# Expert layer of a two-block transformer kernel: upper 256 tokens computed densely, lower 256 by gathered rows

## The reference, cut to what matters

```
s = einsum('thpd,hpnd->thpn', q, sub_keys)          # 128 keys on each of two sides
sc, idx = top_k(s, 16)                              # best 16 of each side
cand = sc[..., 0, :, None] + sc[..., 1, None, :]    # 256 pair sums of a head
top_sc, pos = top_k(cand, 16)                       # best 16 pairs = experts
gate = softmax(top_sc)
act = gelu(einsum('thkd,td->thk', u_tab[eb], hb))   # 128 experts of each token
y = einsum('thk,thkd->td', gb * act, v_tab[eb])
```

## Time and profile before

| what | value |
|---|---|
| median of 3 runs | 3458.14 us (3454.32 to 3459.94) |
| span of the profiled execution, first to last instruction | 3452.1 us |
| busy: PE, DVE, POOL, ACT | 3142.6, 2087.5, 1917.9, 1062.6 us |
| DMA, moved in all | 741.7 MB, of it 536.9 MB by the gathers |
| DMA in the last third of the span | 421 GB/s, all 16 engines busy |

### The profile page before, as it was taken

The page is one execution under the profiler, slowest core; times in us unless marked ns, Lnnn a source line. Parts: engine busy times, 40 slices in busy tenths (PEclk is TensorE's granted clock), DMA queues, the critical chain, the costliest instruction groups (busy, mean ns, idle before and its releaser), DMA issues.

```text
span 3452.1 us, 34902 instructions
## 1 busy us (share of the span) xinstructions
PE 3142.6 (91%) x12254; PEld 2099.6 (61%) x12254; DVE 2087.5 (60%) x3701; ACT 1062.6 (31%) x2577; POOL 1917.9 (56%) x1198
## 2 busy tenths in 40 slices
PE   7999999999999999999999999999978787777776
PEld 5778778887766888868777677544433333333332
DVE  5764453336764433479556776777667676666654
ACT  4564441112165211120132432333333332333222
POOL 4545259997403899968767565444444444434432
PEclk9999999999999999999999999999999999999999
DMA  4430022232311222323413124999999999999997
GB/s 164 171 134 1 13 86 98 97 120 74 134 62 49 90 95 96 115 71 124 140 62 115 50 80 172 421 421 419 422 415 412 421 421 421 421 421 420 421 421 299
DMA packets 108994, 741.68 MB, mean 215 GB/s; under 512 B 11816, under 2 KB 12968, under 8 KB 20776
## 3 DMA queue, kind: packets, MB, share of 16 engines
q0 software_dynamic: 73728, 536.90, 37.5%
q1 hardware_dynamic: 31488, 196.25, 16.2%
q10 hardware_dynamic: 3624, 6.56, 0.5%
HBM read 731.28 MB, written 8.39 MB: 214 GB/s over the span
## 4 chain that ended last, share of the span: by engine, by line
PE 63%; DMA 21%; DVE 8%; ACT 4%; issue 2%; POOL 2%; DVEq 0%; POOLq 0%; ACTq 0%
DMA arena<-in_peer_uv,rstd 15%; PE bank L1298 13%; PE bank L1299 13%; PE bank L1300 13%; PE bank L1814 8%; DMA weight_ring<-in_peer_uv,rstd 3%; DMA normed<-in_peer_uv,rstd 2%; DVE arena L3295 2%; PE bank L1829 1%; PE bank L1744 1%; PE bank L1726 1%; PE bank L1612 1%; PE bank L1490 1%; PE bank L1245 1%; PE bank L1500 1%
## 5 line engine op out<-in xcount | busy, mean ns | idle before, releaser
L1155 POOL DMA_INDIRECT arena<-in_peer_uv,rstd x419 | 456.4, 1089 | 622.0 <-PE bank L1814 570.3
L3295 DVE CUSTOM_DVE_ANT_0 arena<-arena,branch 128x1024 f32<-128x1024 f32 x419 | 510.5, 1225 | 333.5 <-DMA arena<-in_peer_uv,rstd 327.5
L1300 PE MATMUL bank<-split_arena 128*128 128x512 f32 x1776 | 695.1, 391 | 0.0
L1066 POOL TENSOR_TENSOR split_arena<-weight_ring,ones 128x1024 fp32r<-128x1024 f32 x204 | 506.6, 2483 | 151.0 <-PE bank L1300 99.3
L1298 PE MATMUL bank<-split_arena 128*128 128x512 f32 x1392 | 546.6, 393 | 5.6 <-DVE split_normed L2697 2.5
L1299 PE MATMUL bank<-split_arena 128*128 128x512 f32 x1392 | 542.3, 390 | 0.0
L1068 POOL TENSOR_TENSOR split_arena<-weight_ring,split_arena 128x1024 fp32r<-128x1024 f32 x204 | 519.3, 2545 | 16.0
L1814 PE MATMUL bank<-arena,row_diagonals 128*128 128x512 f32 x836 | 397.8, 618 | 92.0 <-ACT row_diagonals L2425 91.7
L1814 PE MATMUL bank<-arena,level_mask 128*128 128x512 f32 x840 | 392.0, 608 | 75.0 <-ACT level_mask L2425 74.7
L1300 PEld LDWEIGHTS bank<-split_arena 128*128 128x128 f32 x1776 | 334.0, 188 | 73.6
L1035 POOL TENSOR_TENSOR split_arena<-weight_ring,split_arena 128x1024 fp32r<-128x1024 f32 x54 | 129.5, 2406 | 401.2 <-ACT split_arena L1980 349.3
(11 more groups left out here) (490 smaller groups left out, 4921.4 us busy)
## 6 DMA issues: line engine op xcount, KB each, us to landing
weight_ring<-in_w_up SPq DMA_DIRECT2D x32, 1024.0 KB, 4.9
weight_ring<-in_w_down SPq DMA_DIRECT2D x32, 1024.0 KB, 4.9
weight_ring<-in_w_in SPq DMA_DIRECT2D x32, 1024.0 KB, 5.0
weight_ring<-in_ada_w SPq DMA_DIRECT2D x24, 1024.0 KB, 4.9
weight_ring<-in_w_in_a SPq DMA_DIRECT2D x12, 1024.0 KB, 6.4
weight_ring<-in_w_out SPq DMA_DIRECT2D x12, 1024.0 KB, 6.9
weight_ring<-in_w_in_b SPq DMA_DIRECT2D x10, 1024.0 KB, 5.9
arena<-in_peer_uv,rstd POOLq DMA_INDIRECT x419
```

Of the source, the lines that this page charges most:

```text
L1066: pool.tensor_tensor(hi, part, bc_mid(ones[:], DT), ALU.mult).then_inc(split_hi, 1)
L1155: pool.indirect_dma_start(row_slots[slot_of[r]], None, a["peer_uv"], bass.IndirectOffsetOnAxis(ap=experts[n % 2][:, c:c + 1], axis=0)).the ...
L1300: return pe.matmul(psum[t.bank][:], hi, a_lo[k], start=False, stop=last)
L3295: dve.tensor_tensor_reduce(row, row, h_tok[:, r // NE, :], 1.0, 0.0, ALU.mult, ALU.add, dots[:, i % 4, j:j + 1]).then_inc(dot_ready, 1)
```

## The change

Blocks 0 and 1 (the lower 256 tokens) still gather rows, 256 in all. Blocks 2 and 3 (the upper 256) are computed against the whole table, which is streamed in 256 *items* of 0.5 MB: 128 items of `u_tab`, transposed (an *up* item: 128 experts by 1024), and 128 of `v_tab` (a *down* item). An up item gives the gelu inputs of 128 experts for 256 tokens (24 fp32r products of 256 columns), a down item adds 128 experts' outputs (12 fp32r products of 512 columns). Most gates are zero; the gate matrix is made from one-hot vectors by small products (64 *gate steps*).

For every item ACT copies the raw data to the high half, and the low half is made by POOL (two items of three) or DVE (every third). Three pairs of halves and four raw buffers rotate.

The order is written out as 320 steps: 64 up items (stage A), 32 gate steps (G0), 128 items in turn down and up (stage B), 32 gate steps (G1), 64 down items (stage C). The first 64 gathered rows are still summed on PE in 32 groups ahead of that (stage S), with all of the queries and 61 pieces of search among them. The other 192 rows are spread over the 320 steps (24 in A, 12 in G0, 96 in B, 12 in G1, 48 in C), and their second half is now added by DVE (`late_add`) in place of PE. Eight searches are left for stage A, one piece a step.

The residual is stored to DRAM and fetched back at the end, since its space holds the split items.

```diff
+        for s, (kind, v) in enumerate(STEPS):        # TensorE
+            if kind == "gate":
+                gate_products(v)
+            elif ITEMS[v][0]:
+                down_unit(v, ITEMS[v][1])
+            else:
+                up_unit(v, ITEMS[v][1])
...
+            def up_unit(n, j):
+                t = u_tiles[j]
+                hi, lo = [x.rearrange("p (k i) -> p k i", i=NKEY) for x in pairs_of[n % PAIRS]]
+                low_wait(pe, n)
+                free(pe, t)
+                for k in range(DT):
+                    pe.matmul(psum[t.bank][:, 0:DENSE], hi[:, k, :], dense_hi[:, k, :], start=k == 0, stop=False)
+                    pe.matmul(psum[t.bank][:, 0:DENSE], hi[:, k, :], dense_lo[:, k, :], start=False, stop=False)
+                    m = pe.matmul(psum[t.bank][:, 0:DENSE], lo[:, k, :], dense_hi[:, k, :], start=False, stop=k == DT - 1)
...
+            def raw_top(n):                          # ScalarE
+                act.wait_ge(raw_landed[n % RAWS], 16 * (n // RAWS + 1))
+                if n >= PAIRS:
+                    act.wait_ge(item_done, n - PAIRS + 1)
+                act.activation(pairs_of[n % PAIRS][0], raws[n % RAWS], ACT.Copy).then_inc(raw_high, 1)
...
+            def raw_rest(n):                         # GpSimd, for two items of three
+                hi, lo = pairs_of[n % PAIRS]
+                pool.wait_ge(raw_high, n + 1)
+                pool.tensor_tensor(lo, raws[n % RAWS], f32(hi), ALU.subtract).then_inc(raw_low[0], 1)
...
+            def weight_rest(m):                      # VectorE
+                w_hi, w_lo = w_parts[m % 2]
+                dve.wait_ge(w_high, m + 1)
+                dve.tensor_tensor(w_lo, weights[:, :, m % WHALF], f32(w_hi), ALU.subtract).then_inc(w_low, 1)
...
+            def late_add(x):
+                row, w = late_slots[gather_slot[x]][:, D:2 * D], late_act[:, x % 8:x % 8 + 1]
+                dve.wait_ge(late_gate, x + 1)
...
+                    m = dve.scalar_tensor_tensor(acc[n], row, w, acc[n], ALU.mult, ALU.add)
...
+            for s, (kind, v) in enumerate(STEPS):    # VectorE
+                for x in rows_at[s - 1] if s else ():
+                    late_add(x)
+                if kind == "gate":
+                    second_ones(v)
+                    if v % NGATE:
+                        gate_weights(v - 1)
...
+                else:
+                    raw_rest(v + 2)
+                    if v in next_weight:
+                        weight_rest(next_weight[v])
+                for x in rows_at[s]:
+                    late_product(x)
+                pieces(s + NGRP)
...
+            for s, (kind, v) in enumerate(STEPS):    # ScalarE
...
+                    if v and not ITEMS[v - 1][0] and v - 1 not in (WHALF - 1, item_of(NKEY - 1, False)):
+                        activate(ITEMS[v - 1][1])
+                    raw_top(v + 2)
+                    if v in next_weight:
+                        weight_top(next_weight[v])
+                for x in rows_at[s]:
+                    late_weight(x)
```

More of the change, by code:

```diff
@@ new lines, in build @@
+        G_FIRST = {0: item_of(0, True), 1: item_of(WHALF, True)}
+        STEPS = []
+        for n in range(2 * NKEY):
+            for half, at in G_FIRST.items():
+                if n == at:
+                    STEPS += [("gate", half * NGATE + q) for q in range(NGATE)]
+            STEPS.append(("item", n))
+        step_of = {x: s for s, x in enumerate(STEPS)}
+        V_LAST = step_of["item", G_FIRST[1]]
+        late_score_at = {10: (1, 2, 6), 18: (1, 3, 7)}
+        index_at = {21: 0, 35: 1}
@@ L576, in build @@
+        v_tiles = [item_tile(2 * NKEY - 1, b) for b in range(4)]
         q_f = region(0, LH)
@@ L922, in build @@
[L922 to L927 removed]
+        next_weight = {item_of(m, True) - (2 if m < WHALF else 1): m for m in range(NKEY) if m % WHALF}
@@ new lines, in build @@
+        G_AT = [step_of["gate", half * NGATE] for half in range(2)]
+        row_step = []
+        for first, last, count_ in ((4, G_AT[0], 24), (G_AT[0], G_AT[0] + NGATE, 12), (G_AT[0] + NGATE, G_AT[1], 96),
+                                    (G_AT[1], V_LAST, 12), (V_LAST, V_LAST + 56, 48)):
+            row_step += [first + i * (last - first) // count_ for i in range(count_)]
+        first_gather = {0: -1, 1: -1, 2: 22, 3: G_AT[0]}
+        gather_step = [first_gather[gather_slot[x]] if gather_prev[x] is None else row_step[gather_prev[x]] + 2 for x in range(LATE)]
@@ L929, in build @@
+        for n, g in SEARCHES[1:]:
+            for _ in range(PIECES if parts[n][g][1] == 2 else 5):
+                search_end[n, g] = next(at)
+                piece_at.setdefault(search_end[n, g], []).append((n, g))
+        exp_at = {e + 1: k for k, e in search_end.items()}
+        norm_at = {e + 3: k for k, e in search_end.items()}
         block = ctx.enter_context(nc.Block())
@@ L1160, in _ @@
+            for x in range(2):
+                late_gather(x)
+            raw_rest(0)
+            raw_rest(1)
+            for s, (kind, v) in enumerate(STEPS):
+                if kind == "item":
+                    raw_rest(v + 2)
+                else:
+                    first_ones(v)
+                for x in gathers_at[s]:
+                    late_gather(x)
         @block.tensor
@@ L3282, in _, with pieces @@
                 pass
-            walk = iter(())
+            walks = {k: search(*k) for k in SEARCHES[1:]}
+            def pieces(w):
+                if w in norm_at:
+                    normalize_gates(*norm_at[w])
+                for k in piece_at.get(w, ()):
+                    next(walks[k], None)
             for i in range(NGRP):
@@ L3312, in _ @@
-            add_rows(TT - 1)
-            finish_rows(TT - 1)
+                pieces(i)
+            for k in range(DT):
+                dve.wait_ge(dense_high, k + 1)
+                dve.tensor_tensor(dense_lo[:, k, :], H[:, k, DENSE:], f32(dense_hi[:, k, :]), ALU.subtract).then_inc(dense_split, 1)
+            for x, t in enumerate(row_sums):
+                full(dve, t)
+                dve.tensor_copy(acc[0][:, 512 * x:512 * (x + 1)], psum[t.bank][:]).then_inc(bank_out[t.bank], 1)
+            for t in row_sums:
+                have(dve, t)
```

640 lines of the change are left out of this document (462 added, 178 removed).

## The result

The changed kernel took 3940.3 us (median of 4 runs, 3938.6 to 3941.9) against 3458.7: a ratio of 1.140 (95% interval 1.138 to 1.141). Slower was right; 3725 us was 215 us too low, and 3940 lies outside the range of 3470 to 3840. Of the rivals' times 3837 comes nearest, for a mechanism that turned out not to be there.

A forecast was written before the change was run, and what follows sets the result against it. It took DMA gathers, 2.49 us a row, to bound the kernel before. Start of A at 2403, plus 275 + 105 + 538 + 105 + 280 + 15, gave 3721, with 6 us added 3727: about 3725 us, range 3470 to 3840.

The forecast's parts named there:

- The gate stages: G0 and G1: 2.7 us a step, 86 us, plus about 19 for 12 rows: 105 us each (bounds 75 to 150).
- Stage C: Down items: 4.7 us for each of 56 steps, 22 us for 8 without rows: 280 us (bounds 212 to 310).
- The lock: VectorE operations with two SBUF inputs and GpSimd's shut each other out: 2 us on 0.667 of steps, less 0.2.
- Stage B: Alternating down and up items: 3.1 us plus 1.1 of lock, 4.2 a step: 538 us (bounds 400 to 600).
- the lock's sign: In the changed profile, VectorE's addition or product averaging 1.8 us or more, and GpSimd's low half over 2.41 us.
- Stage A: Up items with 24 rows: VectorE's 3.9 us plus 0.4, 4.3 a step: 275 us (bounds 237 to 336).
- Stage S: First 64 rows, queries and 61 search pieces, TensorE's and VectorE's loads in different groups: 250 us (bounds 220 to 265).
- Ahead of the layer: Before the layer's first product at 2141 us: nothing changes but one 2 MB store, counted at nothing, at most 5 us.
- TensorE's pitch: Spacing of TensorE's 256-column records in up items: taken as 0.12 us, 2.9 us an item (bounds 2.7 to 5.4).
- rival 3: TensorE bounds after all: 0.227 us pitch at 256 columns, 3837 us; or clock down to 1.2 GHz, 4068; chance 0.12.
- Rival 1: No lock for row products and additions, only plain TENSOR_TENSOR shut out: 3525 us; chance 0.24.
- Rival 2: Faster: buffers let VectorE run without gaps and DMA bounds B (400 us) and C (212): 3398 us; chance 0.12.

The follow-up runs named there:

- e4: The changed kernel with the 192 late rows' gathers, products and additions left out: 3512.4 us, ratio 1.016.
- e1: The changed kernel with GpSimd's eight comparisons of a gate step made one VectorE operation: 3874.0 us, ratio 1.121.
- e10: e7 with VectorE's write of the gates moved behind the next one-hots: 3602.5 us, ratio 1.043.
- e2: The changed kernel with the low halves of all items made by VectorE, none by GpSimd: 3816.4 us, ratio 1.104.
- e3: The changed kernel with the gated weights stored contiguously, the gate step's write strided instead: 3910.4 us, ratio 1.131.
- e5: The changed kernel with GpSimd's low halves replaced by two memsets, which read nothing: 3725.5 us, ratio 1.078.
- e6: The changed kernel with a late row's gelu and gate one step later, its addition two steps after its product: 3866.6 us, ratio 1.118.
- e7: The changed kernel with the edits of e1, e2, e3 and e6 together: 3640.2 us, ratio 1.053.
- e9: e7 with the items' low halves neither made nor multiplied: 3545.1 us, ratio 1.025.
- e11: e10 with only 4 of a gate step's 8 tokens multiplied: 3585.9 us, ratio 1.038.

## Why the prediction was wrong

The differences by stage come to 214 us (-29 + 12 + 86 + 25 + 87 + 40 - 1, and -6). The -6 is the difference between span and time that I added to my sum: this profiled span, 3940.1, is the median's, and every execution whose time and span are both on record lies only 1.7 to 2.1 us above its span. So most of the 6 us between span and median of the kernel before was probably the difference between two of its executions, and not start and end.

- **The gate stages, forecast 105 each, took 191 and 192: the step that failed, 173 us of the miss.** I charged GpSimd's eight comparisons "at about 0.29" from the affine select, one record of another operation, and treated it as known; the bounds that I gave the stage (75 to 150) did not hold twice that price. Measured 0.593 alone, 4.74 a step, 4.84 with the handing on (e4: 155 us without rows, where my working had 86). That is 69 us a stage; the rows add 36 in place of my 19, since GpSimd has their gathers in its own queue (17 us in G0) and its comparisons lengthen beside them (0.69 us in the mean for 0.62 in e4, another 17). With the right price of 0.593 the working would have given 155 + 19 = 174 each.
- The stage had a second fault: my working had no TensorE in it at all. TensorE runs there at a granted clock of 0.50 (1.2 GHz), and its sixteen records take 3.65 us a step, 117 us a stage, which by itself is over my 105. The ring of two buffers gives 163 with GpSimd's comparisons on VectorE (e1) and 145 to 148 at best (e10).
- **Stage C, forecast 280, took 320.** The lock was right and its place wrong. I let GpSimd's low half delay the next row's product; it delays the weights' low half (1683 ns, the product 1283), for which TensorE waits as well (the timeline above). The 64 of the one stand for some 68 us more than alone, the 48 of the other for 2. e2 takes the lock away: 278. The strided operations on the weights, ScalarE's copy at 0.65 for the 0.40 that I took from a contiguous one among them, are worth 10 us (e3). My working gave 285, of which I took 5 off without a reason (and its 3.55 us a step without the lock should read 3.49: 0.857 x 3.9 + 0.143). How the rest of the 40 divides between the lock's place and the chain of copies no run shows.
- **Stage B, forecast 538, took 563** (549 to its last up item). The mechanism was the one forecast, the lock behind a chain between VectorE and ScalarE (4.2 us a step; measured 4.3 to 4.4), and e2, e5 and e6 show it: 481, 455 and 516. But I had charged all of it to the rows' operations; the weights' low half takes as much (1474 for 596 ns in e2, some 56 us in the stage, the products some 45). So the mean of 1.8 us or more that I named as the lock's sign did not come: the product stands at 1646 ns and the addition at 1457. The strided operations are 13 us of the 25 (e3).
- **Stage A, 287 for 275**, near in size. GpSimd's low halves cost more there than the 26 us that I added for them: with GpSimd only writing it takes 241 (e5). That VectorE and its chain set it shows in e2 (284, no gain from the lock's removal, since VectorE then has the low halves too) and in e7 (VectorE busy 256 of 267 us).
- **Stage S, 29 us too long.** The first up item came at 2374. From the first product at 2144 to 2368 TensorE was busy 216.9 of 224 us, close to the 218 us that I had summed for it; I had put VectorE's searches into groups of their own behind it, and they overlapped (VectorE busy 194 of the 224 us). This error made the whole look nearer than it was.
- **Ahead of the layer, the end, and TensorE's pitch** were near: the first product at 2144 for 2141, 14 us for 15, 0.12 us for 0.12. So rival 3 falls for the items (and its 4.5 us a step in B did not follow from its own prices, (5.45 + 2.72) / 2 = 4.09); its half clock came true only in the gate stages. Rival 1 falls by the product's 1646 ns against 1219 and 1217 in e5 and e2. Rival 2's B (400 us) is nearly reached by e7 (413), but not its total.

**Why no version wins.** Of the kernels here the best whole one, e10, takes 3603 us, 4.3% over before; even e9, with a third of the items' products gone, is 2.5% over. Putting together the shortest stages that whole kernels reached (first up item 2372, A 268, G 148 and 145, B 413, C 238, end 14) gives 3598; with A and C of e9 3502. Both are spans, and the span before is 3452. The gates are the price that I underrated: the kernel before has no stage that turns a list of experts into dense gates, and even in e10 these two take 293 us, in which DMA moves 96 and 113 GB/s. Against 421 GB/s that is some 223 us of transfers not made, and stage A, at 226 GB/s for 268 us, is another 124: together 347, more than the 320 us that were on offer. e10 is not the last word on the gate stages: it carries e3's strided write, 0.55 us a gate step of VectorE's time (18 us a stage), and e10 without e3 was not run.

## What to carry to other kernels

A stage that exists only in the changed kernel deserves the widest bounds: price its instructions by operation and operand kind, put every engine of its loop in a row (with the number of buffers), and double the bound where the only row is of another operation. Where GpSimd reads SBUF beside VectorE, look for the instruction of VectorE that becomes ready just after GpSimd's starts: here one of 0.61 us took 2.36, the rest of GpSimd's, and removing waits elsewhere lengthened instructions instead (e6). Work moved from GpSimd to a busier VectorE can pay: here 171 low halves gave back 124 us.

## What was not expected of the hardware

- GpSimd's comparison of 128 columns against a value per partition took 593 ns, the affine select of the same size 289, and VectorE's comparison of all eight at once 1.22 us: a quarter of GpSimd's 4.74.
- TensorE stayed at a granted clock of 0.50 through both gate stages of every kernel, with sixteen back-to-back records of 3.65 us in every 4.6 to 6 us (busy 118 of 201 us), and also at 115 of 148 us (e10) and 62 of 141 (e11). In A, busy 217 of 278 us, it had 0.89.
- A ScalarE copy of 256 columns with a stride of 64 elements took 0.65 us for 0.40, VectorE's low half of the same 0.61 for 0.42. The Trainium skill (SBUF — State Buffer, "Door 1: The DMA port swizzle", the note on SBUF cachelines) says that each access which crosses to a new line pays; e3 agrees, with 404 and 418 ns once the weights are contiguous (the latter in e9, where no lock hides it).
